# Expert loop of a hybrid decoder layer: the wide unit's down weights are copied and loaded at another place in each engine's order

## The chip, the cores and the metric

One core of a Trainium2 chip runs the whole kernel. The metric is the time of one execution on the device in microseconds; the table below gives the median of three runs and the single execution that was profiled. The expert loop has 31 iterations with this input, counted in the trace; every iteration writes to the same buffers.

## The reference, cut to what matters

One decoder layer: a mixer with three branches, then a mixture of experts. The change touches the routed experts alone. 512 tokens of width 1024 go each to 6 of 64 experts with 256 inner channels:

```
def block(inp):
    xb, gb = inp
    a = jnp.einsum('td,edf->tef', xb, w_gate)
    u = jnp.einsum('td,edf->tef', xb, w_up)
    return jnp.einsum('tef,efd->td', jax.nn.silu(a) * u * gb[..., None], w_down)
```

All inputs and the output are float32.

## The kernel before

The kernel is written engine by engine, with semaphores by hand. Each engine executes its own instructions strictly in the order in which they stand; nothing reorders them. After the mixer and the router the tokens of every expert have been packed into units: a wide unit holds up to 128 token rows of one expert, a narrow unit up to 64. One iteration `i` of the expert loop (the `Fori` blocks of each engine) computes one wide and one narrow unit, usually of different experts, so it needs two experts' weights.

**Weights.** A unit's weights are three pieces of 1 MB: the two halves of gate and up (pieces 0 and 1, each loaded by two DMAs, L628) and down (piece 2, one DMA, L632). Every piece has one staging buffer, `w_raw[b][k]`, with b = 0 for the wide and 1 for the narrow unit. A piece of the next unit is loaded as soon as its buffer has been read. All six pieces go through SyncE's queue, in the order of the loop at L645, and land in about that order.

**Precision.** The wide unit's products are made in three terms, from a rounded high half and a low half of each operand. ScalarE makes the high half of the weights with a copy of 128x2048 elements: `gate_hi` (L1787, pieces 0 and 1) and `down_hi` (L1793, piece 2). VectorE subtracts it from the original and gets the low half: `weights_lo` (L2503, all three pieces). When VectorE is through, the staging buffer is free. The halves have one buffer for each piece too: a copy into it has to wait until TensorE has used the last unit's. The narrow unit's products use the staging buffers directly (L1375 gate and up, L1400 down).

**TensorE's order** in an iteration (the code names in brackets): gate and up of narrow unit i (`gate_up_narrow`, L1375), transposes of the next wide unit's gathered tokens (`turn`, L1338), `down` of wide unit i (L1416), transpose of the narrow activations (L1390), `gate_up` of wide unit i+1 (L1358 with the high halves, L1362 with the low ones, once for each half), `down_narrow` (L1400), transposes of the next narrow tokens (L1345) and of the wide activations (L1384). The text counts a cycle from the start of one `down` to the start of the next.

**ScalarE's order** in an iteration: `act_turned` (L1816, the high half of the wide activations), `down_hi`, `gated` for the narrow unit (Silu, L1810), `turned` (L1799, the wide tokens), `gate_hi` of half 0, `store_y` (two copies of the wide outputs, L1827), `gate_hi` of half 1, `act_turned` for the narrow unit, `gated` for the next wide unit (L1810), `turned_narrow` (L1804), `store_narrow` (L1834). VectorE follows with `act_turned` (L2536), `weights_lo` of the down piece, `gated` (L2530), `turned` (L2523), `weights_lo` of halves 0 and 1, `gated` of the next wide unit. GpSimd copies the lists of rows (L797), gathers the next tokens (L784) and scatters the outputs to memory (L811).

The semaphore `down_used` starts at 1 and rises by one at the end of each `down` and each `down_narrow`. `gu_used` counts the gate/up halves of both kinds of unit. `down_lo_ready` counts VectorE's low halves of down weights.

## Time and profile before

| | |
|---|---|
| Median of 3 runs | 1382.17 us (1381.64 to 1382.87) |
| The profiled execution | 1380.12 us |
| Its span in the profile | 1378.2 us |
| TensorE (PE) busy | 1244.9 us, 90% of the span |
| VectorE (DVE) busy | 784.0 us, 57% |
| ScalarE (ACT) busy | 600.5 us, 44% |
| GpSimd (POOL) busy | 298.0 us, 22% |
| Moved by DMA | 314.56 MB, mean 228 GB/s |
| First `down` to last `down` (30 cycles) | 743.97 to 1311.51 us |

The durations below come from the one profiled execution, with times counted from the start of its span. A busy share is a mean over the whole program. "Idle before" is the time in which an engine executed nothing ahead of an instruction, and the name behind the arrow is what ended it. PEclk is the granted share of TensorE's full clock.

### The profile page before, as it was taken

What the parts mean: (1) busy time and instruction counts of PE and PEld (TensorE: products, weight loads), DVE (VectorE), ACT (ScalarE), POOL (GpSimd) and SP (SyncE); (2) the same over time, 40 slices, a digit from 0 to 9 for tenths busy, and PEclk for the clock granted to TensorE, in tenths of its full rate; (3) what the DMA queues carried; (4) which work ended last, traced back from release to release, by engine and by line L of the source; (5) the groups of instructions that cost most, each with busy time, mean ns of one, the idle gap of its engine ahead of it and who ended that gap; (6) DMA issues with size and microseconds to landing.
All of it is one profiled execution on the core that took longest, in us unless ns stands there. A gap on an engine that the chain in (4) does not pass through costs nothing.

```text
span 1378.2 us, 19357 instructions
## 1 busy us (share of the span) xinstructions
PE 1244.9 (90%) x6468; PEld 871.8 (63%) x6468; DVE 784.0 (57%) x1126; ACT 600.5 (44%) x831; POOL 298.0 (22%) x329
## 2 busy tenths in 40 slices
PE   4899999989998899999989999899898998999984
PEld 1597788556554468889956666566665666666642
DVE  1649675769997736445596554345544455444425
ACT  3723522533334552222404566455555455555503
POOL 1200100012410000000002344333433334333313
PEclk9999999899999999999999999999999999999997
DMA  8325222003217152324319999999999999999864
GB/s 309 97 93 184 92 61 87 29 16 107 77 61 262 45 183 92 92 92 161 129 57 356 405 406 388 376 398 404 393 371 373 369 376 351 355 357 361 311 253 199
DMA packets 126633, 314.56 MB, mean 228 GB/s; under 512 B 20277, under 2 KB 57466, under 8 KB 122106
## 3 DMA queue, kind: packets, MB, share of 16 engines
q1 hardware_dynamic: 112250, 288.73, 57.5%
q0 software_dynamic: 14336, 25.20, 5.0%
q8 instruction: 30, 0.49, 0.1%
q14 instruction: 17, 0.14, 0.0%
HBM read 308.62 MB, written 30.41 MB: 246 GB/s over the span
## 4 chain that ended last, share of the span: by engine, by line
PE 53%; DVE 20%; ACT 11%; DMA 9%; issue 6%; SPq 1%; ACTq 0%; POOL 0%; DVEq 0%; POOLq 0%
PE bank L935 16%; DVE arena_parts L2503 9%; PE bank L940 8%; PE bank L1416 6%; DMA ring<-in_exp_w_down 6%; ACT arena_parts L1793 4%; PE bank L1400 3%; ACT arena_parts L1787 3%; PE bank L1362 2%; PE bank L1345 2%; DVE arena L2229 2%; PE bank L1464 2%; DMA arena<-in_ada_w 2%; DVE top L2228 1%; PE bank L882 1%
## 5 line engine op out<-in xcount | busy, mean ns | idle before, releaser
L2503 DVE TENSOR_TENSOR arena_parts<-ring,arena_parts 128x2048 fp32r<-128x2048 f32 x93 | 213.2, 2292 | 118.4 <-ACT arena_parts L1787 67.4
L935 PE MATMUL bank<-hT_parts,ring_parts 128*128 128x512 f32 x344 | 143.6, 417 | 4.9 <-DVE arena L2172 3.5
L935 PE MATMUL bank<-x_parts,ring_parts 128*128 128x512 f32 x344 | 137.5, 400 | 0.0
L1416 PE MATMUL bank<-arena_parts,oTB_parts 128*128 128x512 f32 x372 | 102.2, 428 | 37.8 <-DVE arena_parts L2503 37.8
L1375 PE MATMUL bank<-ring,oTA 128*64 128x256 f32 x992 | 113.9, 382 | 10.2 <-ACT oTA L1804 10.2
L1787 ACT ACTIVATE arena_parts<-ring 128x2048 fp32r<-128x2048 f32 x62 | 118.6, 1912 | 5.1 <-DMA ring<-in_exp_w_up 5.1
L1507 ACT ACTIVATE ring_parts<-ring 128x2048 fp32r<-128x2048 f32 (+1 forms) x38 | 64.8, 1710 | 115.8 <-DMA ring<-in_w_in 74.4
L1416 PEld LDWEIGHTS bank<-arena_parts,oTB_parts 128*128 128x128 f32 x372 | 73.3, 204 | 58.9 <-issue 43.7
L1358 PE MATMUL bank<-arena_parts,oTA_parts 128*128 128x512 f32 x248 | 100.4, 405 | 1.2 <-DVE oTC_parts L2523 1.2
L1375 PEld LDWEIGHTS bank<-ring,oTA 128*64 128x64 f32 x992 | 70.8, 137 | 45.1 <-issue 16.0
L1358 PE MATMUL bank<-arena_parts,oTC_parts 128*128 128x512 f32 x248 | 97.1, 391 | 0.0
L1913 DVE TENSOR_TENSOR ring_parts<-ring,ring_parts 128x2048 fp32r<-128x2048 f32 (+1 forms) x34 | 68.0, 2007 | 49.0 <-ACT ring_parts L1507 48.7
L2536 DVE TENSOR_TENSOR oTB_parts<-bank,oTB_parts 128x256 fp32r<-128x256 f32 x31 | 13.2, 425 | 126.5 <-ACT oTB_parts L1816 88.9
L940 PE MATMUL bank<-hT_parts,ring_parts 128*128 128x512 f32 x344 | 85.0, 389 | 0.0
L935 PEld LDWEIGHTS bank<-hT_parts,ring_parts 128*128 128x128 f32 x344 | 67.1, 195 | 27.2 <-issue 6.4
L797 POOL COPY tok_of<-toks 128x1 int32 (+1 forms) x62 | 29.3, 472 | 246.4 <-PE bank L1345 196.8
L811 POOL DMA_INDIRECT y_dram<-arena,row_of x62 | 61.5, 992 | 75.0 <-POOL row_of L797 26.3
L935 PEld LDWEIGHTS bank<-x_parts,ring_parts 128*128 128x128 f32 x344 | 66.9, 194 | 16.4 <-issue 2.7
L784 POOL DMA_INDIRECT arena<-h_dram,tok_of x62 | 63.7, 1028 | 52.6 <-POOL tok_of L797 52.6
L1810 ACT ACTIVATE oTB<-bank 128x256 f32<-128x256 f32 (+1 forms) x62 | 20.4, 330 | 124.1 <-PE bank L1362 110.0
L1362 PE MATMUL bank<-arena_parts,oTA_parts 128*128 128x512 f32 x248 | 70.5, 406 | 3.1
L940 PEld LDWEIGHTS bank<-hT_parts,ring_parts 128*128 128x128 f32 x344 | 64.6, 188 | 13.4
(451 smaller groups left out, 2370.0 us busy)
## 6 DMA issues: line engine op xcount, KB each, us to landing
ring<-in_exp_w_gate SPq DMA_DIRECT2D x124, 512.0 KB
ring<-in_exp_w_up SPq DMA_DIRECT2D x124, 512.0 KB
ring<-in_exp_w_down SPq DMA_DIRECT2D x62, 1024.0 KB
ring<-in_w_in SPq DMA_DIRECT2D x25, 1024.0 KB, 5.4
ring<-in_ada_w SPq DMA_DIRECT2D x16, 1024.0 KB, 5.7
arena<-in_ada_w SPq DMA_DIRECT2D x4, 2048.0 KB, 16.7
x<-in_x SPq DMA_DIRECT2D x2, 2048.0 KB, 13.3
ring<-in_w_o SPq DMA_DIRECT2D x4, 1024.0 KB, 5.6
```

The costliest lines, as they stand in the source:

```text
L784: g.indirect_dma_start(out=xg[b][0:n], out_offset=None, in_=h_dram[:, :], in_offset=bass.IndirectOffsetOnAxis(ap=rows[0:n] if rows is not ...
L811: g.indirect_dma_start(out=y_dram[:, :], out_offset=bass.IndirectOffsetOnAxis(ap=row_of[b][0:rows, 0:1], axis=0), in_=ys[b][0:rows], in_of ...
L935: mm(out, w if weights_left else t, t if weights_left else w, start=(j == 0 and k == 0), stop=False)
L940: ins = mm(out, w if weights_left else t, t if weights_left else w, start=False, stop=(j == n - 1))
L1358: mm(out_gu, t[:, tile_cols(4 * k + j)], hi[:, :, j, :], start=(k == 0 and j == 0 and x_ == 0), stop=False)
L1362: ins = mm(out_gu, xe_hi[:, tile_cols(4 * k + j)], lo[:, :, j, :], start=False, stop=(k == 1 and j == 3))
L1375: ins = mm(bank[3][r_, 0:FF].rearrange("p (g f) -> p g f", g=2), xe[:, 4 * k + j, :], w[:, :, j, tile_cols(h)], start=(k == 0 and j == 0), ...
L1416: ins = mm(bank[4 + n][:, :], s_, w, start=(q == 0), stop=(q == 5))
L1507: A(hi_view(name, 1, n), ring_view(name, 0, 1, n), ACT.Copy).then_inc(sem("hi_split"), 1)
L1787: A(w_hi[k], w_raw[0][k], ACT.Copy).then_inc(sem("gu_hi_ready"), 1)
L1913: v.tensor_tensor(lo_view(name, 1, n), ring_view(name, 0, 1, n), hi_view(name, 1, n).bitcast(F32), ALU.subtract).then_inc(sem("lo_split"), 1)
L2503: v.tensor_tensor(w_lo[k], w_raw[0][k], w_hi[k].bitcast(F32), ALU.subtract).then_inc(sem("gu_lo_ready" if k < 2 else "down_lo_ready"), 1)
```

## The change

Five things change, all in the expert loop and just ahead of it:

- On ScalarE, `down_hi` of unit i+1 now comes in iteration i, behind `gated` of the wide unit i+1 and ahead of `turned_narrow`. The first unit's comes ahead of the loop. It waits until `down` of unit i is done.
- On ScalarE, both `gate_hi` copies now come ahead of the two output copies of `store_y`.
- On VectorE, `weights_lo` of the down piece moves in the same way, behind `gated` of unit i+1.
- On SyncE, the wide down piece of the next unit is loaded right behind the narrow down piece, ahead of the two narrow gate/up pieces.
- After the loop, neither engine has down weights left to convert.

```diff
--- before.py
+++ after.py
@@ -651,12 +651,12 @@
                 en = expert(1, i)
                 sp.wait_ge(sem("down_used"), 2 * i + 1)
                 load_piece(en, 1, 2)
+                sp.wait_ge(sem("down_lo_ready"), i + 1)
+                load_piece(e, 0, 2)
                 en = expert(1, i + 1)
                 for k in range(2):
                     sp.wait_ge(sem("gu_used"), 4 * i + 2 + k + 1)
                     load_piece(en, 1, k)
-                sp.wait_ge(sem("down_lo_ready"), i + 1)
-                load_piece(e, 0, 2)
             e = expert(1, more)
             sp.wait_ge(sem("down_used"), 2 * more + 1)
             load_piece(e, 1, 2)
@@ -1786,10 +1786,11 @@
                     act.wait_ge(sem("gu_used"), 4 * used + k + 1)
                 A(w_hi[k], w_raw[0][k], ACT.Copy).then_inc(sem("gu_hi_ready"), 1)
 
-            def down_hi(i):
+            def down_hi(i, used=None):
 
                 act.wait_ge(sem("w_loaded02"), 16 * i + 16)
-                act.wait_ge(sem("down_used"), 2 * i + 1)
+                if used is not None:
+                    act.wait_ge(sem("down_used"), 2 * used + 2)
                 A(w_hi[2], w_raw[0][2], ACT.Copy).then_inc(sem("down_hi_ready"), 1)
 
             def turned(i):
@@ -1839,23 +1840,23 @@
             turned(0)
             act.wait_ge(sem("actS_ready"), 2)
             gated(0, 0)
+            down_hi(0)
             turned_narrow(0)
             with act.Fori(0, more) as i:
 
                 act_turned(i, 0)
-                down_hi(i)
                 gated(i, 1)
                 turned(i + 1)
-                gate_hi(i + 1, 0, i)
+                for k in range(2):
+                    gate_hi(i + 1, k, i)
                 store_y(i, 16 * i + 16)
-                gate_hi(i + 1, 1, i)
 
                 act_turned(i, 1)
                 gated(i + 1, 0)
+                down_hi(i + 1, i)
                 turned_narrow(i + 1)
                 store_narrow(i, 16 * i + 16)
             act_turned(more, 0)
-            down_hi(more)
             gated(more, 1)
             store_y(more, 16 * more + 16)
             act_turned(more, 1)
@@ -2540,18 +2541,18 @@
             weights_lo(0, 1)
             shared_act(1)
             gated(0, 0)
+            weights_lo(0, 2)
             with dve.Fori(0, more) as i:
 
                 act_turned(i)
-                weights_lo(i, 2)
                 gated(i, 1)
                 turned(i + 1)
                 weights_lo(i + 1, 0)
                 weights_lo(i + 1, 1)
 
                 gated(i + 1, 0)
+                weights_lo(i + 1, 2)
             act_turned(more)
-            weights_lo(more, 2)
             gated(more, 1)
 
             dve.wait_ge(sem("extra_loaded"), 128)
```

TensorE's instructions stand in the same order as before. On ScalarE, inside the loop, this stood before from the first gate/up copy on (`ring` is the staging memory, `arena_parts` the halves, `bank` TensorE's outputs; L1787 `gate_hi`, L1827 `store_y`, L1810 `gated`, L1804 `turned_narrow`; ISA and REGISTER_ALU compute what a wait compares with):

```order
L1787 ACTIVATE arena_parts<-ring 128x2048
L1827 ACTIVATE arena<-bank 128x512
L1824 REGISTER_ALU
L1827 ACTIVATE arena<-bank 128x512
L1786 REGISTER_ALU
L1787 ACTIVATE arena_parts<-ring 128x2048
L1816 ACTIVATE oTB<-bank 128x128
L1809 ISA
L1810 ACTIVATE oTB<-bank 128x256
L1803 REGISTER_ALU
L1804 ACTIVATE oTA<-bank 128x512
```

And now, where the lines behind L1789 are one or two higher (L1794 is `down_hi`, L1828 `store_y`, L1811 `gated`, L1805 `turned_narrow`):

```order
L1787 ACTIVATE arena_parts<-ring 128x2048
L1822 ISA
L1828 ACTIVATE arena<-bank 128x512
L1825 REGISTER_ALU
L1828 ACTIVATE arena<-bank 128x512
L1817 ACTIVATE oTB<-bank 128x128
L1810 ISA
L1811 ACTIVATE oTB<-bank 128x256
L1791 ISA
L1794 ACTIVATE arena_parts<-ring 128x2048
L1804 REGISTER_ALU
L1805 ACTIVATE oTA<-bank 128x512
```

The second copy L1787 now stands ahead of both output copies, with the first directly before it, and L1794 stands between the wide unit's Silu and the copy of the narrow tokens.

On VectorE the loop began before with these rows (L2536 low half of the activations, L2503 `weights_lo` of the down piece, L2530 `gated` of the narrow unit):

```order
L2543 ISA
L2536 TENSOR_TENSOR oTB_parts<-bank,oTB_parts 128x256
L2502 REGISTER_ALU
L2503 TENSOR_TENSOR arena_parts<-ring,arena_parts 128x2048
L2529 REGISTER_ALU
L2530 TENSOR_TENSOR oTB<-bank,oTB 128x128
```

And now this stands at the loop's end (L2504 `weights_lo`: twice for gate and up, then for the down piece; L2531 `gated` of the next wide unit):

```order
L2501 ISA
L2504 TENSOR_TENSOR arena_parts<-ring,arena_parts 128x2048
L2501 REGISTER_ALU
L2504 TENSOR_TENSOR arena_parts<-ring,arena_parts 128x2048
L2531 TENSOR_TENSOR oTB<-bank,oTB 128x256
L2503 REGISTER_ALU
L2504 TENSOR_TENSOR arena_parts<-ring,arena_parts 128x2048
```

The subtraction for the down weights has moved from the first part of the loop to its end, one unit ahead.

On SyncE the loop ended before with the two narrow gate/up pieces and then the wide down piece (128x2048):

```order
L656 ISA
L628 ISA
L628 DMA ring<-in_exp_w_gate 128x1024
L628 DMA ring<-in_exp_w_up 128x1024
L656 REGISTER_ALU
L628 ISA
L628 DMA ring<-in_exp_w_gate 128x1024
L628 DMA ring<-in_exp_w_up 128x1024
L632 DMA ring<-in_exp_w_down 128x2048
```

And now the wide down piece stands directly behind the narrow one (128x2x1024), ahead of the narrow gate/up pieces:

```order
L632 ISA
L632 DMA ring<-in_exp_w_down 128x2x1024
L632 DMA ring<-in_exp_w_down 128x2048
L635 ISA
L635 TENSOR_LOAD uexp
L635 ISA x2
L658 ISA
```

One DMA has moved ahead of four.

## Rows read from the trace of the kernel before

**Rows 1.** The page: busy tenths of the DMA engines in 40 slices

```profile
DMA  8325222003217152324319999999999999999864
```

**Rows 2.** Timeline, PE, 1200 to 1220 us: start us, us, what [idle before <-releaser]

```profile
1200.93 3.03 PE L1416 MATMUL bank<-arena_parts,oTB_parts 128*128 128x512 f32 x12 [0.97 <-DVE arena_parts L2503]
...
1208.28 0.39 PE L1358 MATMUL bank<-arena_parts,oTC_parts 128*128 128x512 f32 x1
...
1208.78 1.19 PE L1362 MATMUL bank<-arena_parts,oTA_parts 128*128 128x512 f32 x4
...
1213.63 3.67 PE L1375 MATMUL bank<-ring,oTA 128*64 128x256 f32 x32 [0.33 <-ACT oTA L1804]
...
1217.23 1.16 PE L1338 MATMUL bank<-ident,arena 128*128 128x128 f32 x8
...
1219.37 0.95 PE L1416 MATMUL bank<-arena_parts,oTB_parts 128*128 128x512 f32 x3 [0.97 <-DVE arena_parts L2503]
```

**Rows 3.** Timeline, ACT, 1200 to 1222 us

```profile
1200.53 1.92 ACT L1787 ACTIVATE arena_parts<-ring 128x2048 fp32r<-128x2048 f32 x1
...
1204.49 1.91 ACT L1787 ACTIVATE arena_parts<-ring 128x2048 fp32r<-128x2048 f32 x1
...
1210.01 0.38 ACT L1810 ACTIVATE oTB<-bank 128x256 f32<-128x256 f32 x1 [3.44 <-PE bank L1362]
...
1212.90 0.60 ACT L1804 ACTIVATE oTA<-bank 128x512 f32<-128x512 f32 x1 [2.51 <-PE bank L1345]
...
1214.90 1.90 ACT L1793 ACTIVATE arena_parts<-ring 128x2048 fp32r<-128x2048 f32 x1
```

**Rows 4.** Timeline, DVE, 1200 to 1222 us

```profile
1206.43 2.29 DVE L2503 TENSOR_TENSOR arena_parts<-ring,arena_parts 128x2048 fp32r<-128x2048 f32 x1 [1.66 <-ACT arena_parts L1787]
...
1215.04 0.42 DVE L2536 TENSOR_TENSOR oTB_parts<-bank,oTB_parts 128x256 fp32r<-128x256 f32 x1 [4.18 <-ACT oTB_parts L1816]
...
1216.83 2.29 DVE L2503 TENSOR_TENSOR arena_parts<-ring,arena_parts 128x2048 fp32r<-128x2048 f32 x1 [1.37 <-ACT arena_parts L1793]
```

**Rows 5.** Stretches: us, busy us (instructions) by engine, PEclk, DMA share, GB/s

```profile
743.97:875.51 131.54, 119.16 (x669) 81.48 (x667) 63.99 (x57) 76.22 (x101) 50.32 (x57) 1.00 1.02 401
...
1010.21:1068.17 57.96, 51.05 (x285) 34.93 (x286) 27.29 (x25) 32.96 (x43) 22.65 (x25) 1.00 1.01 381
...
1088.00:1144.10 56.10, 51.08 (x286) 34.95 (x286) 27.38 (x25) 32.49 (x43) 22.29 (x24) 1.00 1.00 373
...
1164.10:1293.07 128.97, 119.13 (x665) 81.53 (x666) 63.86 (x57) 73.95 (x99) 50.17 (x56) 1.00 1.00 360
...
875.51:896.40 20.89, 19.59 (x96) 13.76 (x96) 9.03 (x9) 9.76 (x15) 6.69 (x8) 0.85 0.93 358
...
1144.10:1164.10 20.00, 18.59 (x96) 12.80 (x96) 9.03 (x9) 9.77 (x15) 6.68 (x8) 0.91 0.95 346
...
743.97:1144.10 400.13, 363.08 (x1999) 248.97 (x1997) 191.38 (x169) 224.29 (x297) 150.94 (x169) 0.98 1.01 387
...
743.97:1311.51 567.54, 516.73 (x2845) 353.98 (x2844) 273.39 (x241) 317.21 (x420) 216.41 (x241) 0.98 0.99 375
```

**Rows 6.** Waits, 743 to 1312 us: who <- whom, us in total, times, longest

```profile
ACT arena_parts L1793 <- DMA ring<-in_exp_w_down: 5.8, 5, 1.6
```

**Rows 7.** Chain of waits at 1047.79 (start, us, what); timeline, ACT, 1063.68

```profile
1047.79 15.86 DMA ring<-in_exp_w_down
...
1063.68 1.91 ACT L1793 ACTIVATE arena_parts<-ring 128x2048 fp32r<-128x2048 f32 x1 [1.63 <-DMA ring<-in_exp_w_down]
```

**Rows 8.** Timeline, PE: three starts of down, and the idle time before each

```profile
875.51 0.79 PE L1416 MATMUL bank<-arena_parts,oTB_parts 128*128 128x512 f32 x1 [2.60 <-DVE arena_parts L2503]
...
1144.10 1.30 PE L1416 MATMUL bank<-arena_parts,oTB_parts 128*128 128x512 f32 x3 [1.76 <-DVE arena_parts L2503]
...
1029.17 1.19 PE L1416 MATMUL bank<-arena_parts,oTB_parts 128*128 128x512 f32 x4 [1.50 <-DVE arena_parts L2503]
```

**Rows 9.** Timeline, PE, the last down

```profile
1311.51 4.59 PE L1416 MATMUL bank<-arena_parts,oTB_parts 128*128 128x512 f32 x12 [2.06 <-DVE arena_parts L2503]
```


## The prediction

> **What bounds the kernel now.** The program-wide slices show the DMA engines at nine tenths or more from slice 23 on: that is the expert loop, 30 cycles from the first `down` to the last in 567.5 us, and the only stretch that the change touches [rows 1, 5]. I read one late iteration engine by engine first, then the loop by stretches, then the exceptions.
>
> In the late iteration that starts with the matmuls of `down` at 1200.93 and ends at 1219.37, a cycle of 18.44 us, TensorE stands still at two places that matter here [rows 2]. `down` itself waits 0.97 us for VectorE's low halves of the down weights (L2503). Before that, the low-half matmuls of the second gate/up half start at 1208.78, 0.50 us behind the last high-half matmul at 1208.28, where neighbours stand 0.23 us apart: 0.27 us lost, again to L2503. The third stop, 0.33 us before L1375, waits for a copy of the narrow tokens and stays.
>
> ScalarE's rows say why [rows 3]: `down_hi` (L1793) runs from 1214.90 to 1216.80, behind `store_narrow`; VectorE then needs 2.29 us (1216.83 to 1219.12) and `down` starts at once [rows 4]. The second gate/up copy (L1787) starts only at 1204.49, behind the first output copy. ScalarE is idle for 2.51 us before L1804 at 1212.90, and a copy of 1.9 us fits there.
>
> The second bound is data. Each iteration loads six pieces of 1.05 MB, 6.29 MB, plus the gathered and scattered rows. From 744.0 to 875.5 the DMA engines are busy all the time and move 401 GB/s; later stretches give 381, 373 and 360 [rows 5]. In 400.1 us from the first `down` to 1144.1 there are 21 cycles, 19.05 us each, at 387 GB/s, though the engines' own chain would allow 18.44. The excess shows in one form: five copies of down weights waited for the transfer, 5.8 us together [rows 6]. One was issued at 1047.79 and landed 15.86 us later, with ScalarE idle for the last 1.63 us [rows 7]. It had the two narrow gate/up pieces ahead of it in the queue. A gap of 2.60 us before `down` at 875.51, or of 1.76 us at 1144.10, is followed by TensorE's lower level (1.2 GHz instead of 2.4); one of 1.50 us at 1029.17 is not [rows 8]. There are four such cycles; the first and the last take 20.89 and 20.00 us at a granted clock of 0.85 and 0.91, and move only 358 and 346 GB/s [rows 5].
>
> **The change, part by part.** Instructions are the same in number; PE's order is untouched.
>
> *ScalarE, L1793 moved behind the wide gate's Silu.* In the late cycle it would start at about 1210.4 (the Silu of 0.38 us starts at 1210.01) and end at 1212.3, before the 1212.9 at which the narrow token copy can start anyway [rows 3]. Cost nothing while the data are there; its cover is the 2.51 us idle. Queued behind it are L1804, which TensorE waits for, then `store_narrow`. Its new condition, that this iteration's `down` is done, was met at about 1204.
>
> *VectorE, L2503 for the down weights moved up too.* It would end at 1214.7, where VectorE is idle until 1215.04, instead of 1219.12. `down` then follows the transposes of L1338 (1217.23 + 1.16 = 1218.39) directly: 0.97 us saved per clean cycle.
>
> *Both gate/up copies ahead of the output copies.* The second starts 1202.45 instead of 1204.49, so its low half is ready at about 1207.1 in place of 1208.73, even with VectorE's first one (2.29 us) in front: the 0.27 us go. The output copies move from 1203 and 1204 to about 1204.4 and 1205.0; `down_narrow` needs them only behind the L1362 of 1208.78. Cost nothing; with that cover gone, each microsecond would be one on TensorE.
>
> Together a clean cycle goes from 18.44 to 18.44 - 0.97 - 0.27 = **17.2 us**, if the data keep up.
>
> *SyncE.* Its ten DMA issues per iteration stay; the one of the wide down piece moves from the last place to the one behind the narrow down piece, past the four issues of the two narrow gate/up pieces. Its condition is met about 13.5 us after the start of `down` (L2503's end) instead of 18.2 us. It is wanted earlier too: 9.2 us after the next `down`, or 9.8 before L1804 is late, instead of 14.0. Allowance from issue to use: before 18.44 + 13.97 - 18.22 = 14.2 us; after, in a cycle of 18.4, 14.7, and in one of 17.2, 13.5. But it no longer has 2.1 MB of narrow pieces ahead (5.2 us at 401 GB/s), so late down weights should go away. Moved behind it, the narrow pieces wait at most some tenths longer; they have over 15 us until use. The second gate/up half is wanted 2.5 us behind the start of `down` instead of 3.6, and issued only some 0.7 us sooner: its allowance in a cycle of 18.4 falls from 14.0 to 13.7 us, so the first waits are to be expected there.
>
> *What takes the place.* Six megabytes must still come. So I cost the loop by bytes over the rate that each stretch held while fully loaded.
> - To 1144: the cycles at the low clock wasted transfer time. The one at 875.51 moved 20.89 x 358 = 7.48 MB, 18.7 us at 400 GB/s: 2.2 us back. The one at 1144.10, 6.92 MB, 18.55 us at 373: 1.45 back. The two between (20.0 and 19.8 us) give 1.4 and 0.9. Sum 6.0. The rest of the stretch stays at its 18.4 to 19 us, since data set it.
> - From 1164 on: eight cycles of 18.4, seven of them with 360 GB/s, 6.63 MB each, and no wait for data. Bounds: 0, if 360 is all there is, and 8 x 1.24 = 9.9. The nearest loaded stretches did 373 and 381; at 377 a cycle takes 17.6: 8 x 0.83 = 6.6. I take that, since no copy waited for data there.
> - The last `down` has no transposes before it: it waits 2.06 us, and then takes 4.59 instead of 3.03 us, as after the other long gaps [rows 2, 9]. The wait beyond 0.97 is 1.1 and the slow matmuls 1.6: 2.7 saved.
>
> Sum: 6.0 + 6.6 + 2.7 = **15.3 us**. The profiled execution took 1380.12 us (span 1378.2), so 1364.8 on its scale; the median shown is 2.05 higher, which gives 1382.2 - 15.3 = **1366.9 us**.
>
> **A rule weighed against the rows.** The stretch from 744.0 held 401 GB/s [rows 5]. The Trainium skill, DMA: Bandwidth & Descriptors, section Bandwidth, says that for transfers from HBM the HBM side binds at about 358 GB/s, while one core alone may get more. By the 358 the late cycles were full already, which is rival 2; this trace disagrees in its first half (401) and cannot say for its second (360).
>
> **Rivals.**
> 1. *The data rate follows demand.* Cycles come near 17.2 us wherever the load allows. For it: the late stretch ran at 360 GB/s with no copy waiting, so its rate was what was asked for. Against it: the early 21 cycles asked for more than 401 and did not get it. At 400 GB/s throughout, the loop's 567.5 x 375 = 212.8 MB take 532 us: 35.5 saved, with the tail 38: 1344 us.
> 2. *Data are the floor.* The late 360 GB/s are all there is: 6.0 + 2.7 = 8.7 saved, 1373.5 us. If the early stretch also loses to new waits what it gains in clock, the tail alone is left, 1379.5 us, which counts as no change. For it: the DMA share stays at 1.00 late. Against it: with all of the queue's time taken, some copy would have waited late, and none did.
> 3. *Slower: one stop in place of two.* `down_hi` now stands ahead of L1804 in ScalarE's queue, and the gate copies ahead of the stores. If a cycle's whole wait for data gathers in one stop there and passes 1.76 us, the low clock follows (1.6 us), and this in each of the 21 early cycles: 17.2 + 1.8 + 1.6 = 20.6 us against 19.05 is 1.55 x 21 = 32 us lost, less 9.3 late: +23, 1405 us. It decides from stops of about 1.76 us. Against it: the extra stop in a cycle set by data would be (400.1 - 6.0)/21 - 17.2 = 1.6 us in the mean, in several pieces, and a low-clock cycle gives the queue time to catch up, after which it is clean (18.4 us followed three of the four).
> That the change does not do what it says: the order of the instructions shows both moves, so only a late transfer could keep `down_hi` from its place.
>
> **How the numbers follow.** A measurement of this kernel tells about 0.2%, 2.8 us, from nothing. Forecast 0.63, rival 1 0.13, rival 2 0.16 (0.10 of it no change), rival 3 0.08. The forecast's own range, by its bounds (late 0 to 9.9, early 0 to 12), is about 1355 to 1379; the whole range goes from 1350, half way to rival 1, to 1379, and leaves out a fifth. Faster: 0.62 + 0.13 + 0.06 = 0.81; same 0.01 + 0.10 = 0.11; slower 0.08.
>
> **What would show it.** Right: L1416 preceded by under 0.1 us idle in late cycles; TensorE's gap before L1362 gone; L1793 between L1810 and L1804; late cycles of 17.2 to 17.8 us at 370 to 385 GB/s; waits for data at L1787 or L1793, early; no low clock at the last `down`. Wrong: late cycles at 18.4 with 360 GB/s and new waits on DMA (rival 2); early rates above 405 with cycles below 18 (rival 1); a granted clock below 1 in most early cycles (rival 3).

## The result, and the profile after

The changed kernel takes 1371.43 us (median of 11 runs, 1365.29 to 1376.38); the kernel before takes 1381.88 beside it (11 runs, 1374.02 to 1386.43). The ratio is 0.992, with an interval of 0.9903 to 0.9937: 10.5 us less, by the interval 8.7 to 13.4. The forecast was 1366.9, with a range of 1350 to 1379. Two more comparisons gave 1372.52 (0.993) and 1371.84 (0.9922).

The profiled execution of the changed kernel took 1371.31 us with a span of 1369.5; before it was 1380.12 and 1378.2. From the page of the changed kernel: the granted clock, the DMA engines and their rate in 40 slices, the chain that ended last by line, the group of narrow gate/up matmuls, and the issues of two of the loaded pieces (count, size, median us to landing):

```profile
PEclk8799999889999999999998999999999999999997
DMA  8324322003216252224217999999999999999874
GB/s 311 97 94 154 124 62 85 31 16 104 81 51 241 78 184 78 91 93 170 87 60 276 411 401 408 389 401 403 398 386 379 385 378 373 377 370 356 311 297 198
...
DMA ring<-in_exp_w_up 28%; PE bank L935 16%; PE bank L940 8%; PE bank L1375 5%; DMA ring<-in_w_in 2%; DVE arena L2230 2%; DMA arena<-in_ada_w 2%; PE bank L1464 2%; DVE top L2229 1%; PE bank L882 1%; DVE arena_parts L2504 1%; PE bank L1358 1%; PE bank L1362 1%; PE bank L1181 1%; PE bank L1271 1%
...
L1375 PE MATMUL bank<-ring,oTA 128*64 128x256 f32 x992 | 122.2, 392 | 38.0 <-DMA ring<-in_exp_w_up 28.6
...
ring<-in_exp_w_up SPq DMA_DIRECT2D x124, 512.0 KB, 13.6
ring<-in_exp_w_down SPq DMA_DIRECT2D x62, 1024.0 KB, 13.5
```

The line of DMA tenths looks as before [rows 1]: nine or more from slice 23 on. The chain has changed its owner. Its largest item is now a transfer of gate/up weights with 28%. The loop is bound by data.

A clean late cycle of the changed kernel (one without a wait for data; of the seven cycles from 1160.89 to 1287.99 two are so, the others take 17.82 to 19.81 us), TensorE, 1197.07 to 1214.27 (start us, us, what, idle before and its releaser):

```profile
1197.07 3.00 PE L1416 MATMUL bank<-arena_parts,oTB_parts 128*128 128x512 f32 x12
...
1204.80 0.39 PE L1358 MATMUL bank<-arena_parts,oTC_parts 128*128 128x512 f32 x1
1205.03 1.07 PE L1362 MATMUL bank<-arena_parts,oTA_parts 128*128 128x512 f32 x4
...
1209.75 3.67 PE L1375 MATMUL bank<-ring,oTA 128*64 128x256 f32 x32 [0.33 <-ACT oTA L1805]
1213.36 1.16 PE L1338 MATMUL bank<-ident,arena 128*128 128x128 f32 x8
1214.27 2.09 PE L1416 MATMUL bank<-arena_parts,oTB_parts 128*128 128x512 f32 x8
```

It takes 17.20 us, where [rows 2] took 18.44. The 0.97 us before L1416 have gone, and the second L1362 (1205.03) follows the high-half matmul before it by 0.23, not 0.50. ScalarE and VectorE in the same cycle:

```profile
1197.88 3.93 ACT L1787 ACTIVATE arena_parts<-ring 128x2048 fp32r<-128x2048 f32 x2
1201.71 1.07 ACT L1828 ACTIVATE arena<-bank 128x512 f32<-128x512 f32 x2
...
1206.13 0.38 ACT L1811 ACTIVATE oTB<-bank 128x256 f32<-128x256 f32 x1 [3.18 <-PE bank L1362]
1206.41 1.90 ACT L1794 ACTIVATE arena_parts<-ring 128x2048 fp32r<-128x2048 f32 x1
1209.02 0.60 ACT L1805 ACTIVATE oTA<-bank 128x512 f32<-128x512 f32 x1 [0.71 <-PE bank L1345]
```

```profile
1208.35 2.29 DVE L2504 TENSOR_TENSOR arena_parts<-ring,arena_parts 128x2048 fp32r<-128x2048 f32 x1 [1.37 <-ACT arena_parts L1794]
```

`down_hi` (L1794) fills 1.90 of the 2.51 us in which ScalarE stood idle before its narrow copy [rows 3], and 0.71 are left. VectorE is done with the down weights at 1210.64, 3.6 us before `down` wants them.

Stretches of the changed kernel (us, busy us and instructions by engine, granted clock, DMA share, GB/s): the first 21 cycles, these in three parts, cycles 23 to 29, the 30th, in which few weights are left to load, all 30 cycles, and one late cycle with the low clock in it:

```profile
752.89:1143.29 390.40, 357.37 (x1999) 240.59 (x1997) 193.94 (x168) 220.05 (x295) 142.06 (x168) 1.00 1.01 394
752.89:804.54 51.65, 50.24 (x289) 34.82 (x287) 27.64 (x24) 31.02 (x43) 20.21 (x24) 1.00 1.03 406
804.54:1010.81 206.27, 187.35 (x1049) 125.90 (x1047) 101.73 (x88) 115.46 (x155) 74.02 (x89) 1.00 1.02 400
1010.81:1143.29 132.48, 119.78 (x669) 79.87 (x667) 64.57 (x56) 73.57 (x99) 47.83 (x56) 1.00 1.00 380
1160.89:1287.99 127.10, 119.74 (x668) 81.35 (x667) 64.68 (x56) 72.96 (x99) 46.30 (x56) 0.99 1.01 370
1287.99:1304.32 16.33, 15.87 (x90) 10.69 (x88) 8.92 (x7) 9.90 (x13) 5.89 (x7) 1.00 0.65 241
752.89:1304.32 551.43, 509.97 (x2845) 344.11 (x2843) 276.76 (x239) 313.27 (x419) 201.08 (x239) 1.00 1.00 383
1214.27:1234.08 19.81, 18.37 (x99) 12.25 (x97) 9.22 (x8) 10.45 (x15) 6.87 (x9) 0.91 1.01 374
```

The loop went from 567.54 us at 375 GB/s [rows 5] to 551.43 at 383, 16.1 us less. The bytes are the same within 1% (212.8 and 211.2 MB by rate times time). From the first load of expert weights to the last `down` the difference is smaller, 594.2 to 583.0 us, as the first `down` came later. Against [rows 5], stretch by stretch:

| part of the profiled execution | before | after | difference |
|---|---|---|---|
| start to the first load of expert weights (code unchanged) | 717.3 | 721.4 | +4.0 |
| first load to the first `down` | 26.64 | 31.54 | +4.9 |
| first 22 cycles | 420.13 | 408.00 | -12.1 |
| last 8 cycles | 147.41 | 143.43 | -4.0 |
| last `down` to the end | 66.7 | 65.1 | -1.6 |
| span | 1378.2 | 1369.5 | -8.7 |

Waits in the loop of the changed kernel, 752 to 1305 us (who, for whom, us in total, times, longest), those of TensorE's matmuls and those for a transfer:

```profile
PE bank L1375 <- DMA ring<-in_exp_w_up: 28.6, 28, 1.5
...
ACT arena_parts L1787 <- DMA ring<-in_exp_w_up: 11.5, 18, 1.6
...
PE bank L1375 <- ACT oTA L1805: 7.9, 24, 0.3
ACT arena_parts L1794 <- DMA ring<-in_exp_w_down: 4.5, 9, 1.0
```

Before, TensorE lost 37.8 us of the loop waiting for VectorE's down weights, and waited for no transfer at L1375:

```profile
PE bank L1416 <- DVE arena_parts L2503: 37.8, 30, 2.7
```

Now nobody waits at L1416; the narrow gate/up matmuls wait for data, 28.6 us in 28 stops. So the change removed one wait and got most of another in its place. In a data-bound cycle it looks like this (TensorE, 1022 to 1030 us):

```profile
1023.45 0.50 PE L1384 MATMUL bank<-ident,oTB 128*128 128x128 f32 x2
1024.47 1.95 PE L1375 MATMUL bank<-ring,oTA 128*64 128x256 f32 x16 [0.52 <-DMA ring<-in_exp_w_up]
1027.89 1.95 PE L1375 MATMUL bank<-ring,oTA 128*64 128x256 f32 x16 [1.48 <-DMA ring<-in_exp_w_up]
```

The stop of 1.48 us lies between the two halves of L1375, and the second half still runs at full speed (1.95 us for 16 matmuls).

### The profile page after: what moved, and what is told of

The parts are those of the page before. It is cut to its first block, busy times and chain, and to the rows that moved or that the text cites. A ratio compares the mean times of both kernels' runs of the same rounds, so it can differ in the third digit from the quotient of the medians.

```text
span 1369.5 us, 19385 instructions
## 1 busy us (share of the span) xinstructions
PE 1246.1 (91%) x6468; PEld 868.0 (63%) x6468; DVE 787.5 (58%) x1126; ACT 596.8 (44%) x831; POOL 284.1 (21%) x329
## 3 DMA queue, kind: packets, MB, share of 16 engines
HBM read 308.62 MB, written 30.41 MB: 248 GB/s over the span
## 4 chain that ended last, share of the span: by engine, by line
PE 49%; DMA 33%; DVE 10%; ACT 3%; issue 3%; SPq 1%; POOL 0%; ACTq 0%; DVEq 0%; POOLq 0%
DMA ring<-in_exp_w_up 28%; PE bank L935 16%; PE bank L940 8%; PE bank L1375 5%; DMA ring<-in_w_in 2%; DVE arena L2230 2%; DMA arena<-in_ada_w 2%; PE bank L1464 2%; DVE top L2229 1%; PE bank L882 1%; DVE arena_parts L2504 1%; PE bank L1358 1%; PE bank L1362 1%; PE bank L1181 1%; PE bank L1271 1%
## 5 line engine op out<-in xcount | busy, mean ns | idle before, releaser
L2504 DVE TENSOR_TENSOR arena_parts<-ring,arena_parts 128x2048 fp32r<-128x2048 f32 x93 | 211.4, 2291 | 83.9 <-ACT arena_parts L1794 48.3
L1375 PE MATMUL bank<-ring,oTA 128*64 128x256 f32 x992 | 122.2, 392 | 38.0 <-DMA ring<-in_exp_w_up 28.6
L1787 ACT ACTIVATE arena_parts<-ring 128x2048 fp32r<-128x2048 f32 x62 | 118.0, 1918 | 13.8 <-DMA ring<-in_exp_w_up 13.5
L1375 PEld LDWEIGHTS bank<-ring,oTA 128*64 128x64 f32 x992 | 69.0, 140 | 83.0 <-DMA ring<-in_exp_w_up 44.5
L2531 DVE TENSOR_TENSOR oTB<-bank,oTB 128x256 f32<-128x256 f32 (+1 forms) x62 | 22.2, 358 | 168.3 <-ACT oTB L1811 168.3
L1811 ACT ACTIVATE oTB<-bank 128x256 f32<-128x256 f32 (+1 forms) x62 | 20.5, 330 | 205.8 <-PE bank L1375 108.7
L811 POOL DMA_INDIRECT y_dram<-arena,row_of x62 | 75.9, 1224 | 157.5 <-ACT arena L1828 128.0
L1416 PE MATMUL bank<-arena_parts,oTB_parts 128*128 128x512 f32 x372 | 93.2, 399 | 0.0
L797 POOL COPY tok_of<-toks 128x1 int32 (+1 forms) x62 | 55.2, 890 | 162.6 <-PE bank L1345 120.3
L1416 PEld LDWEIGHTS bank<-arena_parts,oTB_parts 128*128 128x128 f32 x372 | 67.6, 188 | 13.5 <-issue 0.4
L1362 PE MATMUL bank<-arena_parts,oTA_parts 128*128 128x512 f32 x248 | 70.9, 408 | 4.7
L784 POOL DMA_INDIRECT arena<-h_dram,tok_of x62 | 63.9, 1030 | 52.6 <-POOL tok_of L797 52.6
L940 PEld LDWEIGHTS bank<-hT_parts,ring_parts 128*128 128x128 f32 x344 | 64.6, 188 | 13.4
## 6 DMA issues: line engine op xcount, KB each, us to landing
x<-in_x SPq DMA_DIRECT2D x2, 2048.0 KB, 13.4
```

Of the source, the lines that this page charges most:

```text
L784: g.indirect_dma_start(out=xg[b][0:n], out_offset=None, in_=h_dram[:, :], in_offset=bass.IndirectOffsetOnAxis(ap=rows[0:n] if rows is not ...
L811: g.indirect_dma_start(out=y_dram[:, :], out_offset=bass.IndirectOffsetOnAxis(ap=row_of[b][0:rows, 0:1], axis=0), in_=ys[b][0:rows], in_of ...
L940: ins = mm(out, w if weights_left else t, t if weights_left else w, start=False, stop=(j == n - 1))
L1362: ins = mm(out_gu, xe_hi[:, tile_cols(4 * k + j)], lo[:, :, j, :], start=False, stop=(k == 1 and j == 3))
L1375: ins = mm(bank[3][r_, 0:FF].rearrange("p (g f) -> p g f", g=2), xe[:, 4 * k + j, :], w[:, :, j, tile_cols(h)], start=(k == 0 and j == 0), ...
L1416: ins = mm(bank[4 + n][:, :], s_, w, start=(q == 0), stop=(q == 5))
```

## The experiments

Theory A: the chain of the engines is 17.2 us per cycle as forecast, and what stands above it is data: the queue's order decides only whose wait it is. Theory B: the new order of the queue makes the narrow pieces late, and that costs time of its own, so the changed engines with the old queue would do better. All ratios are against the kernel before, measured beside the runs of each group.

**The changed kernel again**, in the first and in the third group.

> The changed kernel once more, as the measure for the three runs beside it on the same chip. Theory A (data set the pace: the loop's time is its bytes over about 400 GB/s) and theory B (the engines' chain sets it, and the narrow gate/up piece that now stands behind the wide down piece in the queue takes part of the gain back) both expect what was measured: ratio to before 0.992, about 1371 us, 30 cycles of the loop in about 551 us, and half of the cycles with a wait of 1 to 1.5 us for the narrow unit's second gate/up half.

Measured: 1372.52 us, 0.993 (0.9904 to 0.9956); loop 552.8 us, span 1367.7.

> The changed kernel beside the three runs below on one chip, as their measure: ratio to before 0.992 to 0.993 as in the two comparisons so far, about 1372 us.

Measured: 1371.84 us, 0.9922 (0.9903 to 0.9942); loop 553.3 us, span 1377.1. The loops are the same within 2 us in the three profiles, and so is the time from the first load to the last `down` (583.0, 584.4, 584.9), while the spans differ by 9.4: the first load comes at 718.3 us in one and at 727.1 in this one, in code that the change leaves alone. A single profile tells the loop, but not the whole time to better than some 5 us.

**The engines' order alone** (the changed kernel with SyncE's old order).

```diff
-                sp.wait_ge(sem("down_lo_ready"), i + 1)
-                load_piece(e, 0, 2)
                 en = expert(1, i + 1)
                 for k in range(2):
                     sp.wait_ge(sem("gu_used"), 4 * i + 2 + k + 1)
                     load_piece(en, 1, k)
+                sp.wait_ge(sem("down_lo_ready"), i + 1)
+                load_piece(e, 0, 2)
```

> The changed kernel with SyncE's old order: the wide down piece is issued last again, though its buffer is free some 3 us before. Theory A: the same bytes at the same rate, so the early 21 cycles stay at 18.5 us or more; the waits only move from the narrow unit's matmuls (L1375) to the copy of the down weights (L1794), which has 5.2 us less allowance: 1371 to 1380 us, not faster than the changed kernel. Theory B: the wait at L1375 (28.6 us in all) goes and little takes its place: 1350 to 1362 us.

Measured: 1392.9 us, 1.0071 (1.0045 to 1.0097), slower than before. Both theories missed it, in the same direction. Its stretches and waits:

```profile
752.30:1142.45 390.15, 356.81 (x1904) 242.33 (x1902) 182.69 (x160) 206.88 (x281) 135.14 (x160) 0.94 0.99 377
752.30:1329.10 576.80, 530.82 (x2846) 360.59 (x2844) 273.81 (x239) 309.94 (x419) 208.15 (x241) 0.94 0.98 369
```

```profile
ACT arena_parts L1794 <- DMA ring<-in_exp_w_down: 46.0, 24, 3.6
PE bank L1375 <- ACT oTA L1805: 41.7, 30, 3.2
```

The wide down piece, last in the queue, is late 24 times. ScalarE waits for it ahead of the narrow token copy (L1805), and TensorE waits for that: the mechanism of rival 3. The granted clock over the loop is 0.94. One such stop, TensorE:

```profile
823.35 0.51 PE L1384 MATMUL bank<-ident,oTB 128*128 128x128 f32 x2
825.07 5.36 PE L1375 MATMUL bank<-ring,oTA 128*64 128x256 f32 x32 [1.21 <-ACT oTA L1805]
```

1.21 us behind the transposes, and L1375 takes 5.36 instead of 3.67. Of its 22 stops of 1 us and more at this place, 16 are followed by the low clock. So with `down_hi` ahead of the narrow copy it is the move of the wide piece that makes the move on ScalarE safe, and theory B has fallen. Theory A missed as well: the order of the queue decides more than whose wait it is.

**The queue's order alone** (the kernel before with SyncE's new order; the diff is the reverse of the last one, made to the kernel before).

> The kernel before with SyncE's new order alone; ScalarE and VectorE as before, so the wide down piece is still free only at the end of VectorE's turn, 18.2 us behind the start of down, and the narrow gate/up pieces now queue behind that wait, some 2 to 3.5 us later than before. Theory A: late down weights (5.8 us of waiting, four cycles at the low clock) go, late narrow pieces may take their place; 18.4 us stay the least: 1374 to 1384 us. Theory B: narrow pieces come late in every cycle, since they are issued later: 1384 to 1400 us.

Measured: 1386.09 us, 1.0035 (1.0016 to 1.0055); two us above the upper end of theory A's figure, at the low end of B's. Its loop and the two waits that stop TensorE:

```profile
748.06:1316.58 568.52, 519.27 (x2846) 346.85 (x2844) 276.64 (x241) 313.01 (x420) 165.81 (x241) 0.98 0.99 374
```

```profile
PE bank L1375 <- DMA ring<-in_exp_w_up: 31.2, 36, 1.9
```

The late narrow pieces are there, as in the changed kernel, while the cycle's own chain is still 18.4 us. Five stops of 0.94 to 1.48 us behind transposes were followed by the low clock, six of 1.07 to 1.88 us were not. In the medians each half of the change loses, 0.35% and 0.7%, and the two together gain 0.8%.

**Fewer bytes**, with the changed kernel and with the kernel before: half of each narrow gate/up piece is left unloaded, and the narrow matmuls read the loaded half twice. This takes 1.05 MB from each iteration and leaves the engines' work as it was, but the narrow units then compute another product. The lines are shortened here:

```diff
-  src = a[w][0][...].rearrange("e (p j) f -> (e p) j f", j=8)[:, 4 * k:4 * k + 4, :]
-  sp.dma_start(dst[:, g, :, :], src)
+  src = a[w][0][...].rearrange("e (p j) f -> (e p) j f", j=8)[:, 4 * k:4 * k + (2 if b else 4), :]
+  sp.dma_start(dst[:, g, 0:(2 if b else 4), :], src)
...
-  w[:, :, j, tile_cols(h)]
+  w[:, :, j % 2, tile_cols(h)]
```

> The changed kernel with a quarter of the narrow unit's gate/up rows left out of each load in two (each of the four transfers brings half its bytes, and the narrow matmuls read the loaded half twice): 1.05 MB less per iteration, the same matmuls and copies. Its narrow units compute another product than the reference's. Theory A (data set the pace): every cycle falls to the engines' 17.2 us, the waits at L1375 vanish, 30 cycles in about 515 us against 551, so 1335 to 1342 us. Theory B (the engines' chain with a late piece of its own): the piece still queues last; a third or more of the waits stays: 1350 us or more.

Measured: 1334.57 us, 0.964 (0.9623 to 0.9657).

> The kernel before with the same smaller loads. Theory A: no late down weights, no low clock, 18.43 us in every cycle: 30 cycles in 553 us instead of 567.5, about 1367 us; and between this run and the changed kernel with the same loads lie the engines' own 1.24 us per cycle, 37 us, where the full loads show 10. Theory B: as before less the five late copies, also about 1370 us, but only 15 to 20 us behind the changed kernel with small loads.

Measured: 1374.62 us, 0.9924 (0.9908 to 0.9941). The loops, the changed kernel with fewer bytes and then the kernel before with fewer:

```profile
753.25:1269.49 516.24, 501.98 (x2845) 347.10 (x2843) 276.17 (x239) 309.88 (x419) 204.94 (x239) 1.00 0.96 347
```

```profile
754.04:1306.99 552.95, 509.63 (x2845) 348.43 (x2844) 273.82 (x241) 316.59 (x420) 214.91 (x241) 1.00 0.94 326
```

No matmul of the loop waits for a transfer in either. Every cycle of the second takes 18.40 to 18.46 us. In the first, 29 take 17.20 to 17.25 and the last one 16.31, as the last `down` no longer has its longer wait. The difference is 1.19 us in each of 29 cycles and 2.1 in the last, 36.7 in the loop. This is what the change does to the engines' chain; 1.24 per cycle was forecast. With all its bytes the changed kernel's loop takes 35.2 us more than this (551.4 against 516.2), the kernel before 14.6 more (567.5 against 553.0). So of 36.7 us won on the engines, data take back 20.6 and 16.1 remain, of which 4.9 stand against the later first `down`.

The two medians lie 40 us apart, where theory A had 37 and theory B 15 to 20. The median of the kernel before with fewer bytes lies 7.6 us above theory A's 1367, though its loop is what A said. In its profile the first load comes at 724.7 us, 7.4 later than in the profile of before, once more in the stretch ahead of the loop.

**The gate copies in their old order** (the changed kernel with `store_y` between the two `gate_hi`).

```diff
-                for k in range(2):
-                    gate_hi(i + 1, k, i)
+                gate_hi(i + 1, 0, i)
                 store_y(i, 16 * i + 16)
+                gate_hi(i + 1, 1, i)
```

> The changed kernel with the first output copies between the two gate/up copies again, as before. Theory A: it costs 0.27 us in a cycle only where data leave room (some 12 of 30 cycles, 3 us), and in the others the piece's buffer comes free up to 2 us later, which data-bound cycles feel little: 1371 to 1376 us. Theory B: 0.27 us in each cycle and more, 8 to 12 us: 1380 us or more.

Measured: 1368.87 us, 0.9894 (0.9874 to 0.9914); loop 553.8 us.

> The changed kernel with the output copies between the two gate/up copies, for the second time: its ratio to before was 0.9894 where the changed kernel had 0.992 and 0.993 elsewhere. If the order of the gate/up copies gives nothing, since data set most cycles, both runs here agree within 0.2%. If putting them ahead costs (the scatter of the outputs starts later by two copies), this one is again 3 to 4 us faster than the changed kernel. If it gives its 0.27 us in the cycles with room, this one is 1 to 3 us slower.

Measured: 1370.7 us, 0.9925 (0.9901 to 0.9949); loop 549.7 us. The two loops lie on both sides of the changed kernel's 551.4 to 553.3. From the first load to the last `down` they give 581.6 and 582.5 us, some 2 less. This part of the change is worth nothing that a median or a loop here tells. The likely reason is that the 0.27 us that it saves per cycle on TensorE come back as a wait for data; no run tests that alone. It does move the stops: here they fall more often ahead of the first half of L1375, behind transposes (ten of 1.09 us and more in the first profile, five of them followed by the low clock, and one more of 0.97).

These profiles tell something of the low clock too. The first one's first 22 cycles, and one cycle among them:

```profile
747.97:1158.95 410.98, 381.93 (x2093) 254.72 (x2092) 204.19 (x176) 228.29 (x309) 144.26 (x176) 0.98 1.02 393
952.70:972.28 19.58, 18.48 (x99) 12.25 (x97) 9.31 (x8) 10.39 (x15) 6.50 (x8) 0.91 1.02 408
```

The granted clock over these cycles is 0.98, as it was before the change, with five spells of slow matmuls (four in the second profile). Yet first load to the end of the 22nd cycle takes 438.8 and 440.5 us, where the three profiles of the changed kernel, with no such spell in these cycles, take 439.5 to 441.1. The five cycles of the first profile in which L1375 ran slowly moved 380 to 408 GB/s; the four of the kernel before had moved 346 to 363. So the spells of slow matmuls cost nothing that these profiles show, as the queue stayed full.

**The first unit** (the changed kernel with the narrow copy ahead of `down_hi` before the loop only).

```diff
-            down_hi(0)
             turned_narrow(0)
+            down_hi(0)
             with act.Fori(0, more) as i:
```

> The changed kernel with one edit: ahead of the loop ScalarE copies the narrow tokens first and the down weights after. In the changed kernel the first narrow matmuls start 1.1 us later than that copy would allow, and TensorE's low clock follows (5.23 us instead of 3.67). Both theories: that stop falls to 0.3 us; 1.1 us saved if the low clock comes anyway, 2.7 us if it goes too: 1368.5 to 1370.5 us where the changed kernel has 1371. If the first stretch is covered by something else: no difference.

Measured: 1369.15 us, 0.991 (0.9876 to 0.9944); first load to first `down` 26.63 us, as before the change (26.64), loop 554.3, the two together 581.0.

> The changed kernel with the first down copy behind the narrow tokens' copy ahead of the loop, for the second time: the stretch from the first expert load to the first down was 26.6 us in its profile against 31.5 and 31.6. 2.7 us of it come from this edit, the rest from the clock ahead of the loop: 1.1 to 2.7 us faster than the changed kernel, so 1369 to 1371 us.

Measured: 1373.63 us, 0.9938 (0.9916 to 0.996); first load to first `down` 30.0, loop 553.4, together 583.4. The first unit of the changed kernel, ScalarE and TensorE:

```profile
744.29 1.90 ACT L1794 ACTIVATE arena_parts<-ring 128x2048 fp32r<-128x2048 f32 x1
746.09 0.59 ACT L1805 ACTIVATE oTA<-bank 128x512 f32<-128x512 f32 x1
```

```profile
744.91 0.50 PE L1384 MATMUL bank<-ident,oTB 128*128 128x128 f32 x2
746.82 5.23 PE L1375 MATMUL bank<-ring,oTA 128*64 128x256 f32 x32 [1.41 <-ACT oTA L1805]
```

And of the first run of this experiment:

```profile
739.85 3.67 PE L1375 MATMUL bank<-ring,oTA 128*64 128x256 f32 x32 [0.30 <-ACT oTA L1805]
```

At the first unit `down_hi` holds the narrow copy up: the stop is 1.41 instead of 0.30 us, and L1375 then took 5.23 instead of 3.67, together 2.7 us (the rest of the 4.9 lies before it, mostly in router matmuls at L1271, 3.78 instead of 1.99 us, which the change doesn't touch). But they are not won by this edit. The loop is longer by about as much as the first `down` is earlier: 554.3 behind a start of 26.6, 551.4 behind 31.5, 549.7 behind 32.8 (the second profile of the edit above). The starts of the changed kernel and of these edits differ by 6 us, and the two together, 581.0 to 584.9, by 4. Transfers run from the first load on, and while TensorE is late they get ahead: behind the start of 31.5 the third cycle takes 17.20 us, behind that of 26.6 it takes 19.26. The medians say the same: 1369.15 and 1373.63 lie on both sides of the changed kernel's 1371.4 to 1372.5.

**`down_hi` behind the narrow copy everywhere, and the old queue.** This takes away the place at which the engines-only kernel stopped. The edit in the loop is shown; the same two lines change places ahead of it, and SyncE's lines are those of the engines-only kernel.

```diff
-                down_hi(i + 1, i)
                 turned_narrow(i + 1)
+                down_hi(i + 1, i)
```

> The changed kernel with ScalarE's down copy one place further back, behind the copy of the narrow tokens, in the loop and ahead of it, and with SyncE's old order. A late down piece then no longer stops the narrow matmuls, but down itself, as in the kernel before. Theory A: the bytes are the same, so cycles of 18.5 us in the early stretch; what counts is how often the stops lie behind transposes (L1338) and bring the low clock: 1368 to 1385 us, between the changed kernel and the one with SyncE's old order alone (1393). Theory B: with both old waits gone and the narrow pieces early again it should be the fastest: 1355 to 1365 us.

Measured: 1376.16 us, 0.9939 (0.9924 to 0.9953), 16.7 us less than with `down_hi` ahead and the same queue (0.9939 against 1.0071, in two groups of runs). Its loop and waits:

```profile
751.35:1309.91 558.56, 510.36 (x2846) 357.06 (x2844) 270.43 (x241) 310.33 (x420) 198.34 (x240) 0.98 1.00 379
```

```profile
ACT arena_parts L1794 <- DMA ring<-in_exp_w_down: 40.4, 21, 3.6
PE bank L1416 <- DVE oTB_parts L2537: 37.1, 21, 3.4
```

The down weights are as late as in the engines-only kernel (40.4 us in 21 waits, against 46.0 in 24). But the wait stands at another place, and the loop is 18.2 us shorter, with a clock of 0.98 instead of 0.94. (VectorE's L2537 stands behind L2504 in its queue, so its name is in the row.) Only the places of two copies on ScalarE differ, so which stop the late data make, far more than how late they are, decides between 1392.9 and 1376.2. That the low clock is how it does so is argued: 16 spells of slow matmuls took 28.7 us more than at full clock in the one loop and 6 took 9.4 in the other, which is about the 18.2 us, but slow matmuls alone cost nothing in the kernels with the old gate order. There the queue stayed full; in the engines-only kernel it did not (DMA share 0.98, 369 GB/s). The changed kernel is ahead of this one by 4 to 6 us from the first load to the last `down` (588.6), while the intervals of the ratios overlap (0.9903 to 0.9937, 0.9924 to 0.9953).

**The last two edits together** (gate copies in the old order, the first unit's narrow copy first).

> Both edits together, as the candidate for the fastest version: down copies and loads as in the changed kernel, the first down copy behind the narrow tokens' copy, the gate/up copies as before. The sum of the two effects: 1366 to 1370 us, if the gate order costs something in the changed kernel; 1369 to 1371 us, if it is neutral.

Measured: 1372.25 us, 0.9921 (0.9893 to 0.995). Start 29.4, loop 555.3, together 584.7. Of the kernels that compute the same, none beats the changed kernel by more than the runs can tell.

## Why the prediction was right, and where its steps were not

**Sign and size.** 10.5 us came, of the 15.3 forecast; 15.3 lies outside the interval (8.7 to 13.4), the time is inside the range.

**The clean cycle of 17.2 us: right**, by the late cycle at 1197.07 and by the kernels with fewer bytes, 17.20 to 17.25 against 18.43. `down_hi` in the idle time of ScalarE costs nothing there, as said.

**Data take the place of the wait: right.** With the queue always taken, the time goes by bytes over rate. Counted from the first load, where the transfers begin, the three terms compare as follows, in the profiled execution.

| term | forecast | measured |
|---|---|---|
| first load to the 22nd cycle's end | -6.0 | +4.9 - 12.1 = -7.2 |
| last 8 cycles (6.6), with the last wait (1.1) | -7.7 | -4.0 |
| tail, slow matmuls | -1.6 | -1.6 |
| sum | -15.3 | -12.8 |

By the other two profiles of the changed kernel the sum is 11.4 and 10.9 (first load to last `down` 584.4 and 584.9), next to the 10.5 of the medians.

**The early term: right in size, its cause only in part.** The text put the 6.0 us at transfer time that four cycles lost at the low clock, 346 to 363 GB/s against 368 to 395 in the cycles beside them. That loss has gone, and so has the low clock (granted 1.00 against 0.98). But the clock is not what decides: with the gate copies in their old order the clock is 0.98 again, the queue stays full through the slow cycles, and the time is the same. Which of the moves keeps the queue full is not tested by itself. Part of the 12.1 is only the other side of the 4.9: three cycles ran at 17.2 while the queue had its lead (51.65 us at 406 GB/s, against 55.55 for the first three before).

**The late term: mis-sized, 7.7 forecast, 4.0 measured.** This is the step that failed in the sum: "at 377 a cycle takes 17.6: 8 x 0.83 = 6.6". The rate was 370 GB/s, not 377, and the gain lay elsewhere than the term had it. The seven cycles still loaded fell from 128.97 to 127.10 us, 0.27 each and 1.9 in all, with new waits for data at L1375 (4.4 us in 5); the other two profiles give 1.8 and 1.4. The last one, with 241 GB/s, fell from 18.44 to 16.33 by the engines' chain alone: 2.1 us. In the seven loaded cycles rival 2, with its 0, was nearer than the forecast, with its 0.83. The one cycle of 19.81 us at a clock of 0.91 doesn't explain it: the other two profiles have no slow matmuls there, and their seven cycles take 127.2 and 127.5 us. Why the rate goes from 400 to 380 to 370 in the course of the loop, with the DMA engines taken throughout, no run tells; the kernel before falls in the same way [rows 5].

**The tail: right.** The last L1416 takes 3.02 us where [rows 9] had 4.59, with no stop before it:

```profile
1300.72 3.67 PE L1375 MATMUL bank<-ring,oTA 128*64 128x256 f32 x32 [0.33 <-ACT oTA L1805]
1304.32 3.02 PE L1416 MATMUL bank<-arena_parts,oTB_parts 128*128 128x512 f32 x12
```

**The range.** By the text's own bounds the forecast's lower end is 1382.2 - (9.9 + 12 + 2.7) = 1357.6, not 1355, and the early 12 has no working. This changes nothing in the sum.

**Failed: "cost nothing" for `down_hi`, applied to all units.** The 2.51 us of cover were read in the loop, where TensorE's narrow down matmuls (L1400) of the unit before keep ScalarE's narrow copy waiting. At the first unit there is no such work: ScalarE would have been idle for 0.58 us, and a copy of 1.90 was put there. It cost 1.1 us and, in the three profiles of the changed kernel, 1.6 more of slow matmuls (two experiments with the same stop of 1.41 us kept 3.67). The sum lacked this, and needed it as little: the data had the time to get ahead, and the loop gave it back.

**Failed: where the waits would come.** The text expected them at ScalarE's copies, L1787 above all, and said of the narrow pieces that they "wait at most some tenths longer; they have over 15 us until use". L1787 waited 11.5 us in 18 waits, mostly without stopping TensorE. The 28.6 us that stop it are the narrow pieces', which now come last in the queue: each piece's lateness is decided by all that stands ahead of it, and I weighed only the piece that moved. It was harmless to the sum, as the sum went by bytes.

**Rival 3: the mechanism is real, the threshold was wrong.** It did not come in the changed kernel, since the wide down piece is no longer late (4.5 us in 9 waits). With the old queue it came, and that kernel was slower than before. "It decides from stops of about 1.76 us" was read from stops before `down` [rows 8]; before L1375 stops from 0.89 us on were followed by the low clock. What I took for a length is to a good part a place (below).

**Rival 1** had its sign, a rate above 405 with cycles below 18, in three cycles only (406 GB/s, 17.2 us), while the queue had its lead; the rest of the early stretch held 400 and 380.

**Not settled.** The first load came at 717.3 us in the profile of before and between 717.7 and 727.1 in the others, the experiments included, so that one profile lies at the early end. Its code is the same everywhere. Whether this stretch is moved by anything but chance is open; the figures from the first load on don't depend on it. Why the late rate is 370 GB/s and not the 377 that I had taken is not explained either.

## What to carry to other kernels

When an engine's chain has some slack of data beneath it, find both prices before moving anything: a run with fewer bytes shows the chain alone (36.7 us here), and what comes through goes by bytes over the rate of a loaded stretch, counted from the first load (11.2 here). The piece that is last in the queue is the late one: ask which stop it makes. Each half of the change alone lost here (0.7% and 0.35%). The two together gained 0.8%, and so, nearly, did the old queue with the copy one place further back (0.6%). A step that is free in the loop has to be costed anew at the first and the last iteration, where its cover may be missing.

## What the runs showed of the hardware

**Around L1375 the place of a stop told more about the clock than its length.** I counted TensorE's stops of 1.0 us and more before or within L1375 in the profiles of the changed kernel and of the experiments. Of 86 stops of 1.02 to 1.88 us between two parts of L1375, none was followed by slow matmuls (83 of them come from five profiles of nearly the same kernel). Of 66 stops between the small transposes (L1345, L1384) and L1375, of 1.00 to 3.21 us, 38 were; among the 56 that are as long as the others, 1.02 to 1.88 us, 30. Four shorter ones, of 0.89 to 0.99 us, were too. In the changed kernel itself this one:

```profile
1226.12 0.51 PE L1384 MATMUL bank<-ident,oTB 128*128 128x128 f32 x2
1227.91 5.32 PE L1375 MATMUL bank<-ring,oTA 128*64 128x256 f32 x32 [1.29 <-DMA ring<-in_exp_w_up]
```

Length alone doesn't decide at that place either: 28 such stops, up to 1.88 us, left the clock as it was, and before `down` one of 3.40 us did, in the kernel with `down_hi` behind the narrow copy, where one of 2.00 did not. The Trainium skill, TensorE: Matmul & The Clock Gate, section on the PE-mode transpose, says that transposes do not count as activity of the engine in the way other matmuls do. The counts around L1375 agree with it; the stop of 3.40 us before `down`, which also stands behind transposes (L1338), does not. No run here took the transposes away, so the cause is not shown.

**One core held over 400 GB/s.** 406 GB/s over 51.65 us and 400 over 206.27 us, most of it read from HBM (308.62 MB read and 30.41 written over the whole program), is over the 358 at which the Trainium skill's page DMA: Bandwidth & Descriptors (section Bandwidth) sees the HBM side bind; the page allows one core alone more. The late stretch of the changed kernel held 370 where the kernel before had 360 [rows 5], so those 360 were not quite the limit; yet the seven loaded cycles became only 0.27 us shorter each.
